# Two of a quad's four weight sums made by accumulating DMAs instead of by VectorE, in the Strassen-Winograd part of an fp32 feed-forward layer

## The reference

```python
u = rmsnorm(h, norm_ff_pre[l])
f = jnp.square(jax.nn.relu(u @ w_ff1[l])) @ w_ff2[l]
h = h + rmsnorm(f, norm_ff_post[l])
```

## Time and profile before

| | before |
|---|---|
| median of 3 runs | 1325.41 us (1325.34 to 1327.75) |
| the profiled execution | 1325.52 us, its span 1323.7 us |
| mean granted TensorE clock | 0.998 of full speed |
| TensorE busy with matmuls | 1311.4 us, 99% of the span |
| VectorE busy | 928.1 us, 70% |
| ScalarE busy | 671.0 us, 51% |
| mean HBM traffic | 190 GB/s over the span |

### The profile page before, as it was taken

The page is one execution under the profiler, slowest core; times in us unless marked ns, Lnnn a source line. Parts: engine busy times, 40 slices in busy tenths (PEclk is TensorE's granted clock), DMA queues, the critical chain, the costliest instruction groups (busy, mean ns, idle before and its releaser), DMA issues.

```text
span 1323.7 us, 18258 instructions
## 1 busy us (share of the span) xinstructions
PE 1311.4 (99%) x6998; PEld 1116.4 (84%) x6998; DVE 928.1 (70%) x1265; ACT 671.0 (51%) x922; POOL 47.0 (4%) x92
## 2 busy tenths in 40 slices
PE   9999999999999999999999999999999999999998
PEld 8889999888888888889987888877888877888886
DVE  7766565687875555557768976579876699776554
ACT  7554453456664443454645664445454455545442
POOL 1222110000000000000000000000000000000000
PEclk9999999999999999999999999999999999999999
DMA  9766555555566666674755666646576465766653
GB/s 315 205 185 170 170 163 149 167 167 155 170 194 188 185 188 221 226 246 148 219 159 188 214 219 191 195 156 207 190 223 189 146 207 191 229 188 190 223 195 104
DMA packets 135209, 252.56 MB, mean 191 GB/s; under 512 B 8275, under 2 KB 45551, under 8 KB 134748
## 3 DMA queue, kind: packets, MB, share of 16 engines
q1 hardware_dynamic: 131216, 241.40, 58.6%
q0 software_dynamic: 2160, 4.74, 1.8%
q10 hardware_dynamic: 1756, 5.36, 1.1%
HBM read 249.29 MB, written 2.17 MB: 190 GB/s over the span
## 4 chain that ended last, share of the span: by engine, by line
PE 90%; DVE 6%; ACT 2%; DMA 1%; issue 0%; ACTq 0%; SPq 0%; DVEq 0%
PE bank L2006 16%; PE bank L1696 11%; PE bank L1698 11%; PE bank L1697 11%; PE bank L2009 8%; PE bank L1742 4%; PE bank L2056 4%; PE bank L2057 4%; PE bank L2058 4%; PE bank L1730 3%; PE bank L1731 3%; PE bank L1729 3%; PE bank L1744 2%; DVE b_lo L1536 2%; DVE s_lo L1541 1%; ACT b_hi L873 1%
## 5 line engine op out<-in xcount | busy, mean ns | idle before, releaser
L1017 DVE TENSOR_TENSOR w_lo<-raw,w_hi 128x1024 fp32r<-128x1024 f32 (+1 forms) x360 | 430.6, 1211 | 247.6 <-ACT w_hi L559 246.1
L559 ACT ACTIVATE w_hi<-raw 128x1024 fp32r<-128x1024 f32 (+1 forms) x360 | 372.4, 1048 | 292.9 <-DMA raw<-in_w_ff 173.5
L2006 PE MATMUL bank<-f_hl,w_hi 128*128 128x512 f32 x960 | 229.7, 391 | 0.0
L2006 PEld LDWEIGHTS bank<-f_hl,w_hi 128*128 128x128 f32 x960 | 176.4, 188 | 34.1
L2009 PEld LDWEIGHTS bank<-f_hl,w_lo 128*128 128x128 f32 x960 | 123.1, 191 | 4.7
L2009 PE MATMUL bank<-f_hl,w_lo 128*128 128x256 f32 x960 | 124.5, 283 | 0.0
L1696 PE MATMUL bank<-w_hi,u_hl 128*128 128x512 f32 x256 | 101.1, 395 | 0.0
L1698 PE MATMUL bank<-w_hi,u_hl 128*128 128x512 f32 x256 | 99.9, 390 | 0.0
L1697 PE MATMUL bank<-w_lo,u_hl 128*128 128x512 f32 x256 | 99.8, 390 | 0.0
L873 ACT ACTIVATE b_hi<-b_raw 128x2048 fp32r<-128x2048 f32 x24 | 46.1, 1921 | 72.7 <-DVE b_raw L1528 72.7
L1730 PE MATMUL bank<-u_hl,w_lo 128*128 128x272 f32 x288 | 82.4, 289 | 0.4 <-DVE w_lo L1017 0.4
(11 more groups left out here) (282 smaller groups left out, 2314.7 us busy)
## 6 DMA issues: line engine op xcount, KB each, us to landing
raw<-in_w_ff SPq DMA_DIRECT2D x160, 512.0 KB, 4.0
raw<-in_w_in SPq DMA_DIRECT2D x128, 512.0 KB, 3.7
s_raw<-in_w_ff SPq DMA_DIRECT2D x48, 512.0 KB, 3.9
b_raw<-in_w_ff SPq DMA_DIRECT2D x24, 1024.0 KB, 5.1
raw<-in_w_out SPq DMA_DIRECT2D x32, 512.0 KB, 4.3
raw<-in_w_branch_b SPq DMA_DIRECT2D x16, 512.0 KB, 3.8
raw<-in_w_branch_a SPq DMA_DIRECT2D x16, 512.0 KB, 3.8
xt<-in_turned_x SPq DMA_DIRECT2D x8, 272.0 KB, 5.4
```

The costliest lines, as they stand in the source:

```text
L559: act.activation(w_hi[:, u, :, 0:width], raw[:, u, :, 0:width], ACT.Copy).then_inc(hi_ready, 1)
L1017: dve.tensor_tensor(w_lo[:, u, :, 0:width], raw[:, u, :, 0:width], w_hi[:, u, :, 0:width].bitcast(F32), ALU.subtract).then_inc(lo_ready, 1)
L2006: ins = pe.matmul(acc[g][:], w_hi[:, u, k, cols], f_hl[:, kt, :], start=kt == 0, stop=kt == KT - 1)
```

## The change

Slots 3 and 4 of a quad are no longer computed by VectorE. SP loads the quad's 1 MB as before and, in a second transfer of 256 KB, one more copy of the fourth block into slot 4. When both have landed, GpSimd issues two accumulating DMAs of 256 KB each, which read two other blocks of the quad again from HBM and add them to slots 3 and 4 in SBUF. They count up a new semaphore, `b_added`. VectorE's item "sum" is gone from `LO_ORDER`; its item "sums" now waits for `b_added`. The sums are now additions where they were differences, and the signs are put into the token sums and into `join`, with as many instructions of the same shapes as before. ScalarE's "first" waits for both loads.

```diff
-LO_ORDER = [("sum", 0), ("sums", 0), ("first", 0), ("rest", 0), ("S", 0), ("S", 1), ("sum", 1), ("sums", 1), ("first", 1),
+LO_ORDER = [("sums", 0), ("first", 0), ("rest", 0), ("S", 0), ("S", 1), ("sums", 1), ("first", 1),
...
-    LO_ORDER += [("sum", _k), ("S", 2 * _k - 1), ("sums", _k), ("first", _k), ("rest", _k), ("S", 2 * _k)]
+    LO_ORDER += [("S", 2 * _k - 1), ("sums", _k), ("first", _k), ("rest", _k), ("S", 2 * _k)]
...
                 sp.dma_start(b_raw[k % 2][:, 0:4, :].rearrange("p (k h) n -> p k (h n)", k=2),
                              unit_of(w_ff2, bass.ds(q * D + 4 * j * P, 2 * P), slice(c * 1024, c * 1024 + 1024)))\
+                  .then_inc(b_landed[k % 2], 16)
+                sp.dma_start(b_raw[k % 2][:, 4, :], w_ff2[0, bass.ds(q * D + (4 * j + 1) * P, P), slice(c * 1024 + CW, c * 1024 + 1024)])\
                   .then_inc(b_landed[k % 2], 16)
...
+            for q in range(QUARTERS - 1):
+                for k in range(N_W):
+                    pool.wait_ge(b_landed[k % 2], 32 * (k // 2 + 1 + q * N_W // 2))
+                    _, c, j = ORDER[W_AT[k]]
+                    row, col = q * D + 4 * j * P, c * 1024
+                    pool.dma_start(b_raw[k % 2][:, 3, :], w_ff2[0, row:row + P, col + CW:col + 1024], accum_op=ALU.add)\
+                        .then_inc(b_added[k % 2], 16)
+                    pool.dma_start(b_raw[k % 2][:, 4, :], w_ff2[0, row + P:row + 2 * P, col:col + CW], accum_op=ALU.add)\
+                        .then_inc(b_added[k % 2], 16)
...
-                    act.wait_ge(b_landed[n % 2], 16 * (n // 2 + 1) + q * (16 * N_W // 2))
+                    act.wait_ge(b_landed[n % 2], 32 * (n // 2 + 1 + q * N_W // 2))
...
-                dve.tensor_tensor(work[:, 8, :], work[:, 3, :], work[:, 1, :], ALU.add).then_inc(hid_part, 1)
+                dve.tensor_tensor(work[:, 8, :], work[:, 3, :], work[:, 1, :], ALU.subtract).then_inc(hid_part, 1)
...
-                dve.tensor_tensor(work[:, 10, :], work[:, 0, :], work[:, 9, :], ALU.subtract).then_inc(hid_ready, 1)
+                dve.tensor_tensor(work[:, 10, :], work[:, 0, :], work[:, 9, :], ALU.add).then_inc(hid_ready, 1)
...
-                if kind == "sum":
-                    dve.wait_ge(b_landed[i], 16 * (n // 2 + 1) + q * (16 * N_W // 2))
-                    dve.tensor_tensor(raw_b[:, 4:2:-1, :], raw_b[:, 3:0:-2, :], raw_b[:, 2:4, :], ALU.subtract)\
-                       .then_inc(b_part, 1)
-                elif kind == "sums":
-                    dve.wait_ge(b_part, part + 1)
-                    dve.tensor_tensor(raw_b[:, 5, :], raw_b[:, 1, :], raw_b[:, 4, :], ALU.subtract).then_inc(b_part, 1)
-                    dve.wait_ge(b_part, part + 2)
-                    dve.tensor_tensor(raw_b[:, 6, :], raw_b[:, 0, :], raw_b[:, 5, :], ALU.subtract).then_inc(b_ready, 1)
+                if kind == "sums":
+                    dve.wait_ge(b_added[i], 32 * (n // 2 + 1 + q * N_W // 2))
+                    dve.tensor_tensor(raw_b[:, 5, :], raw_b[:, 1, :], raw_b[:, 4, :], ALU.add).then_inc(b_part, 1)
+                    dve.wait_ge(b_part, n + 1 + q * N_W)
+                    dve.tensor_tensor(raw_b[:, 6, :], raw_b[:, 0, :], raw_b[:, 5, :], ALU.add).then_inc(b_ready, 1)
```

More of the change, by code:

```diff
@@ L319, in hybrid_block @@
         b_landed = [sem(f"b_landed{i}") for i in range(2)]
+        b_added = [sem(f"b_added{i}") for i in range(2)]
         s_landed = [sem(f"s_landed{i}") for i in range(3)]
@@ L1518, in split_item @@
                 lo, hi, raw_b = b_lo[i], b_hi[i], b_raw[i]
-                part = 2 * n + q * (2 * N_W)
-                if kind == "sum":
-                    dve.wait_ge(b_landed[i], 16 * (n // 2 + 1) + q * (16 * N_W // 2))
-                    dve.tensor_tensor(raw_b[:, 4:2:-1, :], raw_b[:, 3:0:-2, :], raw_b[:, 2:4, :], ALU.subtract)\
-                       .then_inc(b_part, 1)
-                elif kind == "sums":
-                    dve.wait_ge(b_part, part + 1)
-                    dve.tensor_tensor(raw_b[:, 5, :], raw_b[:, 1, :], raw_b[:, 4, :], ALU.subtract).then_inc(b_part, 1)
-                    dve.wait_ge(b_part, part + 2)
-                    dve.tensor_tensor(raw_b[:, 6, :], raw_b[:, 0, :], raw_b[:, 5, :], ALU.subtract).then_inc(b_ready, 1)
+                if kind == "sums":
[3 more added lines that the diff above has]
+                    dve.tensor_tensor(raw_b[:, 6, :], raw_b[:, 0, :], raw_b[:, 5, :], ALU.add).then_inc(b_ready, 1)
                 elif kind == "first":
@@ L1565, in join @@
                                       for b in range(BLOCKS) for h in range(2)]
-                dst, other = ((c11, p1), (p6, p1), (p7, p6), (c21, p7), (p6, p5), (c12, p6), (p7, p5), (c22, p7))[step]
+                dst, one, other = ((c11, c11, p1), (p6, p6, p1), (p7, p7, p6), (c21, c21, p7), (p6, p5, p6), (c12, c12, p6),
+                                   (p7, p5, p7), (c22, c22, p7))[step]
                 if step:
                     dve.wait_ge(p_part, step)
-                ins = dve.tensor_tensor(dst, dst, other, ALU.add).then_inc(p_part, 1)
+                dve.tensor_tensor(dst, one, other, ALU.subtract if step in (4, 6) else ALU.add).then_inc(p_part, 1)
                 if step == 7:
```

## The result

The changed kernel takes 1404.08 us (median of 4 runs, 1401.33 to 1407.36) against 1325.38 for the kernel before: a ratio of 1.059, with a 95% interval of 1.0564 to 1.0616. It is 79 us slower. The forecast was 1347 us, with a range of 1332 to 1375. The direction was right; the size was not.

What follows compares the result with a forecast made beforehand. TensorE, busy for 99% of the span, was taken to bound the kernel. Losses of 6.7 us in quarter 1 and 7.5 each in quarters 2 and 3, together 21.8, on 1325.5 gave 1347 us, range 1332 to 1375.

Steps and rivals of the forecast that it cites:

- W0's chain: Quad 0's load to TensorE's W0 at each quarter's opening, held by nothing else; forecast 4.84 us longer.
- the fifth block: The 256 KB load behind each quad's 1 MB; forecast to land about 0.6 us later, with 0.37 us more issue on SP.
- W3 and W7: W items in each quarter forecast to wait 1 to 2 us for "rest": W3 loses 1.7 us, W7 1.4.
- signs of being wrong: A under 4.6 or over 7.3 us, ordinary loads landing later beside the accumulates, or VectorE's instructions longer while GpSimd issues.
- A: Time from both loads' landing to both accumulates' landing; forecast 5.5 us for quad 0, 6.0 in later quads.
- my own rule of 12 us per us of A: Above A = 6.0 us, W0 and links W1-W3-W5-W7 pay in full: 4 us a quarter, 12 in all.
- the sum: Forecast losses over the three quarters: 6.7 us in quarter 1, 7.5 each in quarters 2 and 3, together 21.8 us.
- The `hid_lo_ready` hold: A wait in SP's queue ahead of quad 3's load that passes later; forecast to cost W3 0.3 us more.
- The landing of the later quads' loads: In the steady-state chain, landing after SP's issue: 5.15 us plus 0.6 for the fifth block.
- The relief at W1 and W2: VectorE's queue, shortened by dropping "sum", removes the losses of W1 and W2: 1.2 us a quarter.
- The slow accumulate: Rival, chance 0.17: accumulates much slower than plain transfers, A of 8 to 10 us; 1392 us at A = 9.6.
- the fit of the prediction: GpSimd transfer taken as 2.0 us plus bytes over 436 GB/s; by it the sum is some 15 us smaller.

Runs made afterwards that it cites:

- The filled runs: Changed kernel with 27 discarded matmuls ahead of W0's first wait: 1397.81 us; with 19 more ahead of W3 and 4 ahead of W7: 1394.81 us.

## Why the prediction was right or wrong

**Right.** TensorE's steady flow is what time is made of, and W0's chain has no slack: with the accumulates at the first quad alone, the loss is 31 us, some 5 of them the fifth load's. With the fifth block quad 0 lands 5.5 to 5.8 us after issue, 0.4 to 0.7 later than before (0.6 was forecast). The `w_ff1` stretches, the token sums and `join` cost nothing. W1 began without a gap in all three quarters. W3 and W7 waited for their weights, but for 6 to 8.5 us and 2.5 to 4, not 1 to 2, and W2, W5 and W6 waited too. Two of my own signs of being wrong came in: A over 7.3 us, and ordinary loads landing later.

**The step that failed.** It is the value of A: "A = 4.8 + 0.7 = 5.5 us for quad 0, where nothing else is moving". Something else was moving: quad 1's load, which SP issues 8.3 us after quad 0's, 2.3 us after the first accumulate's issue, when their bytes have just begun to move. I had that row in hand (a pair of issues over 8.72 us in the earlier trace rows) and used it only to say that W1 is safe. Held back, it lets A fall from 8.2 to 6.0 us. That this is near my 5.5 is luck: the row I took A from is of plain transfers with short runs, and plain copies of these blocks gave 4.0, while adding costs the DMA engines about twice the time of a copy, which I put at nothing in the forecast. Both together, the slow adding and the load beside it, make the 8.2. By my own rule of 12 us per us of A, A = 8.2 would have given 1375 us. The 29 us above that are the terms that follow.

**What the sum did not have.** The clock: 17.6 us, which no row of before shows; TensorE's longest waits in its stretches were under 1 us. I priced idle time as idle time alone. The filled runs show that the matmuls behind a wait are lost too, at 0.2 us each for 5 to 13 matmuls.

**Mis-sized terms.** The `hid_lo_ready` hold was put at 0.3 us. SP issued quad 3's load 1.5, 2.0 and 3.2 us after W1's last matmul had begun, where it is 0.4 to 0.6 with the wait moved, and moving it gives back 16 us. (That late loads and late accumulates feed each other from W1 to W3 would explain so much, but is not shown.) The landing of the later quads' loads was left at 5.15 + 0.6 us; with other transfers on the same engines it was 7.5 to 9.7 us for quads 1, 3, 4, 6 and 7, and the S loads took 5.4 us for 3.9. The relief at W1 and W2 was right in size (1.2 us a quarter forecast; without the fifth load their waits fall by 1.0), but the fifth load, priced at W0 alone, took it back. A slip of the sum changes nothing: by my own rule A = 3.3 us makes the sum 17.5 us smaller, not some 15.

**The rivals.** The slow accumulate was nearest, with A of 8 to 10 us and 1392 us: A was 8.2, 7.6 and 8.1 us at quad 0 and 5.8 to 10.3 later. It was there as two transfers one behind the other, and as engines near their limit; the second is what the runs bear out (a DMA share of 0.7 in the stretches, 0.88 between 934 and 954 us). That its 1392 us are near 1404 is partly luck: its rule gives 1375 for the A measured, and it had neither the clock nor the fifth load's full price. The Trainium skill's page "DMA: Bandwidth & Descriptors", section "Anatomy of one DMA — SWDGE (gpsimd) path", has the fit of the prediction, an estimate of 2.6 us for 256 KB and of 3.3 for A. The copies at quad 0 landed 3.2 and 3.4 us after their own issue and made A 4.0; that fit does not price an addition.

## What to carry to other kernels

Before costing a new transfer by the landing time of a similar one, lay it on the timeline and name every transfer issued within its length: here a load issued 2.3 us later added 2.2 us to two accumulates, and its own bytes delayed those behind. A chain that feeds TensorE from an empty queue is the first place to look at, however full the helping engine looks over the stretch, and a wait of 2 us or more on it cost more than itself here, since the clock came back late (9 to 13 matmuls later at the quarters' openings). Price an edit's small companions (one more load, a queue's in-order wait) by a run of their own: the fifth load alone cost as much as the whole relief could give.

## What the runs showed of the hardware

- Accumulating DMAs from GpSimd used the 16 engines for 40 us more than copies of the same 12.6 MB (some 76 us for 36), and were issued in 0.85 and 1.19 us instead of 0.54. Alone on the engines they kept them 0.7 to 0.9 busy at 90 to 213 GB/s.
- One accumulate of 256 KB landed 4.2 us after its issue, with a load issued 2.2 us behind it; two with no load beside them in 6.0; two beside a load of 1.25 MB in 8.2; one of 512 KB beside that load in 6.2.
- After 6 us without work TensorE ran its next 9 to 13 matmuls at 1.2 GHz (0.43 us each instead of 0.2285), and after 2.1 to 2.5 us and a second wait three matmuls later, 6 to 10; kept busy by matmuls with no use, it ran none at 1.2 GHz.
- A GpSimd addition of 1024 columns in SBUF took 2.7 us on average and lengthened VectorE's instructions beside it, one of them from 1.23 to 2.89 us.
